# Gated tiles written in place, branch work dealt out anew, and the matrix state read ahead of the gating

## What is computed

```python
pool_y, pool_new = pool_mixer(cols(OFF_POOL, BRANCH_W), ...)      # branch 0
sb_y = stick_breaking(q_sb, k_all, v_all, pos0)                   # branch 1: 8 heads of 128
h_ml, c_new, n_new, m_new = mlstm_chunkwise(q_ml, k_ml, v_ml, ...)# branch 2: 4 heads of 256
for bi, yb in enumerate((pool_y, sb_y, ml_y)):
    gated = yb * silu(cols(OFF_Z + bi * BRANCH_W, BRANCH_W))
    term = sigmoid(cols(OFF_GATE + bi * D_MODEL, D_MODEL)) * (gated @ w_branch[bi])
    merged = term if merged is None else merged + term
y = merged @ w_out
x_out = x + rmsnorm(y, g_post)
```

## Time and profile before

| | |
|---|---|
| median of 3 runs | 2428.11 us (2427.13 to 2431.63) |
| the profiled execution's own time | 2423.55 us |
| its span | 2422.0 us |
| PE busy in the span | 2274.7 us, 94% |
| DVE, ACT, POOL busy | 61%, 38%, 10% |
| PE's share of the chain that ended last | 86% |

### The profile page before, as it was taken

One profiled execution on the slowest core, in us unless ns is written; L12 is line 12 of the kernel. 1 busy time (PEld: TensorE's weight loads), 2 busy tenths in 40 slices (PEclk: granted clock), 3 DMA queues, 4 the chain that ended last, 5 costly groups with the idle time before them and its releaser, 6 DMA issues.

```text
span 2422.0 us, 40440 instructions
## 1 busy us (share of the span) xinstructions
PE 2274.7 (94%) x16616; PEld 2233.8 (92%) x16616; DVE 1471.9 (61%) x1636; ACT 923.9 (38%) x1232; POOL 244.4 (10%) x301
## 2 busy tenths in 40 slices
PE   3799999999999999999999999999997898699996
PEld 3799999999999999999999999999886788699996
DVE  5867678667666666676666666655663666243333
ACT  4344334334433344444444444445541233122221
POOL 3100000000100001110000000003442111000000
PEclk7899999999999999999999999999997999899998
DMA  5244434444544444444444444466555553635322
GB/s 148 58 120 116 133 101 118 131 117 131 125 115 122 124 117 117 124 123 114 129 126 115 119 124 117 117 212 203 174 183 170 188 162 118 170 104 183 86 70 95
DMA packets 417613, 316.01 MB, mean 130 GB/s; under 512 B 11309, under 2 KB 376997, under 8 KB 415472
## 3 DMA queue, kind: packets, MB, share of 16 engines
q1 hardware_dynamic: 397456, 250.12, 37.4%
q0 software_dynamic: 20000, 63.61, 7.5%
HBM read 252.42 MB, written 61.26 MB: 130 GB/s over the span
## 4 chain that ended last, share of the span: by engine, by line
PE 86%; DVE 6%; DMA 4%; ACT 2%; issue 1%; POOL 1%; SPq 0%; DVEq 0%; ACTq 0%; POOLq 0%
PE pp L685 62%; PE pp L819 10%; PE pp L987 7%; DMA gt_lo<-gated_scratch 2%; PE M L693 2%; PE M L872 1%; PE M L902 1%; DMA raw_b<-in_w_out_dram 1%; PE M L919 1%; PE M L842 1%; PE M L785 1%; PE M L852 1%; DVE den L1867 1%; DVE xa L1427 1%; DVE XA L1750 0%
## 5 line engine op out<-in xcount | busy, mean ns | idle before, releaser
L685 PE MATMUL pp<-xa,wa_hi 128*128 128x288 f32 x7680 | 1543.6, 296 | 26.6 <-DVE wa_lo L1384 14.8
L685 PEld LDWEIGHTS pp<-xa,wa_hi 128*128 128x128 f32 x7680 | 1235.2, 188 | 29.0 <-DVE xa L1427 10.8
L685 PE MATMUL pp<-xa,wa_lo 128*128 128x288 f32 x3840 | 1131.6, 295 | 0.0
L685 PEld LDWEIGHTS pp<-xa,wa_lo 128*128 128x128 f32 x3840 | 725.9, 189 | 0.0
L1384 DVE TENSOR_TENSOR wa_lo<-raw_a,wa_hi 128x1024 fp32r<-128x1024 f32 x274 | 340.6, 1246 | 253.6 <-ACT wa_hi L1025 253.5
L1025 ACT ACTIVATE wa_hi<-raw_a 128x1024 fp32r<-128x1024 f32 x274 | 289.1, 1056 | 225.4 <-PE pp L685 218.6
L1384 DVE TENSOR_TENSOR wa_lo<-raw_r,wa_hi 128x1024 fp32r<-128x1024 f32 x136 | 173.2, 1273 | 141.6 <-ACT wa_hi L1025 141.6
L819 PE MATMUL pp<-gt_hi,wb_hi 128*128 128x288 f32 x768 | 171.9, 306 | 37.6 <-DMA gt_lo<-gated_scratch 37.6
L1025 ACT ACTIVATE wa_hi<-raw_r 128x1024 fp32r<-128x1024 f32 x136 | 143.5, 1055 | 133.5 <-PE pp L685 133.5
L819 PE MATMUL pp<-gt_hi,wb_lo 128*128 128x288 f32 x768 | 166.4, 299 | 0.0
L819 PE MATMUL pp<-gt_lo,wb_hi 128*128 128x288 f32 x768 | 166.4, 299 | 0.0
(11 more groups left out here) (278 smaller groups left out, 2137.3 us busy)
## 6 DMA issues: line engine op xcount, KB each, us to landing
raw_a<-in_w_in_dram SPq DMA_DIRECT2D x206, 512.0 KB, 5.0
raw_r<-in_w_in_dram SPq DMA_DIRECT2D x68, 512.0 KB, 4.9
z_scratch<-zs POOLq DMA_DIRECT2D x60, 576.0 KB, 3.3
raw_b<-in_w_branch_dram SPq DMA_DIRECT2D x48, 512.0 KB, 4.2
raw_b<-in_w_out_dram SPq DMA_DIRECT2D x32, 512.0 KB, 4.4
gz<-z_scratch SPq DMA_DIRECT2D x48, 288.0 KB, 4.0
gt_hi<-gated_scratch SPq DMA_DIRECT2D x6, 1152.0 KB, 10.3
gt_lo<-gated_scratch SPq DMA_DIRECT2D x6, 1152.0 KB, 13.1
```

The costliest lines, as they stand in the source:

```text
L685: i = nc.tensor.matmul(out, ws[:, slot, k, :], xa[:, o, part, k, :], start=opens and k == 0 and s == 0, stop=k == HK - 1 and s == 2, skip_ ...
```

## The change

- Tiles 6 and 7 of branch 1 and of branch 2 no longer go through DRAM. ACT and DVE write them into `gt_hi`, `gt_lo` (`gated_hi_direct`, `gated_lo_direct`), once the last segment of the branch before is done. `seg(16, 1)` and `seg(32, 1)` wait for them one by one; `gated(1, 1)` and `gated(2, 1)` load two tiles in place of four.
- A new semaphore `gt_free` counts the first halves: `seg(15, 0)` and `seg(31, 0)` raise it, and `gated(1, 0)`, `gated(2, 0)` wait for it and no longer for all segments of the branch. To make that early, the last two tiles of a branch run as (14, 0), (15, 0), (14, 1), (15, 1), and likewise 30 and 31.
- The segments are dealt out anew (`SB_SEGS`, `ML_SEGS`, `ML_SLOTS`): one stands ahead of head 0's transposes, head 1 comes after three in place of four, one segment each stands ahead of the last `weigh_values` and `sums_after` of head 6 and 7. The ML heads get 8, 8, 7, 7 segments, and head 3 has none behind its state products.
- `states` becomes a buffer of its own name at the place of `W_ml`. DVE copies the new state before the gating, `decay_rows(i)` moves to the start of head i and waits for the stores of the state, and the two splits of a head's gated tiles move into the next head. ACT's exponential of `W_ml` moves behind the copies to `mk_hi`.
- POOL masks `W_ml` first, then stores the last head's gated tiles, then multiplies `zml` and `oml`.
- In the last 16 tiles the splits of the first two tiles of the output projection move ahead of the last two merges.

```diff
+SB_SEGS = [(h, s) for h in range(H_POOL, H_SB - 2) for s in range(2)] + [(14, 0), (15, 0), (14, 1), (15, 1)]
+ML_SEGS = ([(16, 1), (17, 1)] + [(h, s) for h in range(H_SB + 2, H_ML - 2) for s in range(2)]
+           + [(30, 0), (31, 0), (30, 1), (31, 1)])
+ML_SLOTS = [[2, 1, 1, 2, 1, 1], [2, 1, 1, 2, 1, 1], [2, 1, 1, 1, 1, 1], [2, 1, 1, 2, 1, 0]]
...
+        states = sb("states", R + 82944, [P, 2 * MC * MDH])
-        states = num[:, :, :].rearrange("p c t -> p (c t)")
...
             def gated(b, s):
+                k0, k1 = 4 * s, KW - 2 if s and b else 4 * s + 4
...
-            sp.wait_ge(wb_used, H_SB)
+            sp.wait_ge(gt_free, 1)
             sp.wait_ge(g_stored, 32 * (PG + 4))
             gated(1, 0)
+            merge_gate(18)
+            weights(19)
+            head_past_v(SBH - 1)
+            sp.wait_ge(wb_used, H_SB)
+            sp.wait_ge(g_stored, 32 * (PG + SB_STORED))
+            gated(1, 1)
             merge_gate(19)
...
+            sp.wait_ge(gt_free, 2)
+            sp.wait_ge(g_stored, 32 * (PG + SB_STORED + 4))
+            gated(2, 0)
             sp.wait_ge(wb_used, H_ML)
-            sp.wait_ge(g_stored, 32 * (PG + SBH + 4))
-            gated(2, 0)
-            sp.wait_ge(g_stored, 32 * (PG + SBH + 2 * MLH))
+            sp.wait_ge(g_stored, 32 * (PG + SB_STORED + ML_STORED))
             gated(2, 1)
...
+                direct = {H_SB: PG + SBH, H_ML: PG + SBH + MC * MLH}
                 for k in range(4 * s, 4 * s + 4):
+                    if h in direct and k >= KW - 2:
+                        pe.wait_ge(glo_ready, direct[h] - (KW - 1 - k))
...
+            def gated_hi_direct(k, h, tile, src):
+                act.wait_ge(g_ready, k + 1)
+                act.wait_ge(wb_used, h)
+                nc.scalar.activation(gt_hi[:, tile, :], src, ACT.Copy).then_inc(ghi_ready, 1)
...
+                if i:
+                    k = MC * i - 1
+                    gated_hi(PG + SBH + k, PG + SB_STORED + k, zml[:, 1, :])
...
+            def gated_lo_direct(k, tile, src):
+                dve.wait_ge(ghi_ready, k + 1)
+                nc.vector.tensor_tensor(gt_lo[:, tile, :], src, gt_hi[:, tile, :].bitcast(F32), ALU.subtract
+                                        ).then_inc(glo_ready, 1)
...
             for t in range(KD):
-                h = H_ML + t + 2
-                if h < H_OUT:
-                    split_lo(At(h))
+                split_lo(At(H_ML + t + 2))
                 merge(H_ML + t)
                 if t >= 2:
                     merged_lo(t - 2)
-            split_lo(At(H_OUT))
-            split_lo(At(H_OUT + 1))
...
             def ml_head(i):
+                pool.wait_ge(W_ready, i + 1)
+                apply_mask(W_ml, ML_MASKED).then_inc(Wm_ready, 1)
+                if i:
+                    for c in range(MC):
+                        store_gated(PG + SBH + MC * (i - 1) + c, 2 * KW + MC * (i - 1) + c)
                 pool.wait_ge(mo_loaded, 16 * (i + 1))
                 pool.wait_ge(mg_loaded, 16 * (i + 1))
                 nc.gpsimd.tensor_tensor(zml[:, :, :], zml[:, :, :], oml[:, :, :], ALU.mult).then_inc(zg_ready, 1)
```

More of the change, by code:

```diff
@@ L139, in product_at, with ml_segs, ml_halves @@
     return p.times(7, 2 + j)
+def ml_segs(i, step):
+    at = sum(sum(x) for x in ML_SLOTS[:i]) + sum(ML_SLOTS[i][:step])
+    return ML_SEGS[at:at + ML_SLOTS[i][step]]
+def ml_halves(i, steps):
+    done = []
+    for step in steps:
+        done += [h for h, s in ml_segs(i, step) if s == 1]
+    return done
 def stored_before(p):
@@ L563, in _ @@
             ml_o(0)
-            for i in range(SBH):
+            head_past_k(1)
+            weights(4)
+            for i in range(1, SBH):
                 if i + 1 < SBH:
                     head_past_k(i + 1)
-                weights(2 * i + 4)
-                if 2 * i + 3 >= 4:
-                    merge_gate(2 * i + 3)
+                weights(2 * i + 3)
+                merge_gate(2 * i + 2)
+                if i == 1:
+                    head_qk(2)
                 if i + 2 < SBH:
@@ L624, in _ @@
             ml_c0(0)
+            ml_z(0)
             for i in range(MLH):
@@ L876, in sums_after, with next_seg @@
                               for j in range(NT)]).then_inc(after_done, 1)
-            for i in range(SBH):
+            segs = iter(SB_SEGS)
+            def next_seg():
+                seg(*next(segs))
+            next_seg()
+            keys_to_tokens(0)
+            next_seg()
+            scores(0)
+            next_seg()
+            keys_to_tokens(1)
+            next_seg()
+            scores(1)
+            next_seg()
+            sums_after(0)
+            next_seg()
+            for i in range(2, SBH):
                 keys_to_tokens(i)
-                seg(2 * i, 0)
+                next_seg()
                 scores(i)
[L882 to L888, removed]
+                next_seg()
+                weigh_values(i - 2)
+                next_seg()
+                sums_after(i - 1)
+                next_seg()
+            next_seg()
             weigh_values(SBH - 2)
+            next_seg()
+            sums_after(SBH - 1)
             seg(H_SB, 0)
-            sums_after(SBH - 1)
             seg(H_SB + 1, 0)
@@ L1808, in decay_rows, with merges @@
                 last.then_inc(D_ready, 1)
+            def merges(i, *after):
+                for h in ml_halves(i, after):
+                    merge(h)
+            KTR, SCORES, VTR, WEIGH, SSQ, STATE = range(6)
             def ml_head(i):
                 h = H_SB + 4 * i
-                steps.begin(0, 5)
+                steps.begin(0, 3 + MC)
+                decay_rows(i)
                 dve.wait_ge(mkhi_ready, i + 1)
@@ L1884, in ml_head @@
                                                ).then_inc(state_ready, 1)
+                dve.wait_ge(zg_ready, i + 1)
+                for c in range(MC):
+                    steps.link(nc.vector.tensor_tensor(num[:, c, :], num[:, c, :], den[:, :], ALU.mult))
+                    nc.vector.scalar_tensor_tensor(zml[:, c, :], num[:, c, :], hnorm[:, i * MC + c:i * MC + c + 1],
+                                                   zml[:, c, :], ALU.mult, ALU.mult).then_inc(g_ready, 1)
                 steps.end(1)
-                gated_lo(PG + SBH + MC * i + 1, zml[:, 1, :])
-                merge(h + 3)
-            decay_rows(0)
             for i in range(MLH):
                 ml_head(i)
+            for c in range(MC):
+                gated_lo_direct(PG + SBH + MC * (MLH - 1) + c, ML_STORED + c, zml[:, c, :])
+            merges(MLH - 1, STATE)
             def merged_lo(t):
```

198 lines of the change are left out of this document (99 added, 99 removed).

## The result

The changed kernel takes **2386.12 us** (median of 4 runs, 2384.08 to 2388.48), the kernel before, on the same chip, 2429.87 us (4 runs, 2427.13 to 2434.62): a ratio of 0.982, interval [0.981, 0.983], so 1.8% or 44 us faster. The forecast was 2381 us, in a range of 2369 to 2394. The profiled execution took 2387.73 us where the sum of the prediction had 2376.5: 11.2 us more, and nearly all of it sits in one term.

A forecast was written before the change was run, and what follows sets the result against it. PE was taken to bound the kernel, with gains only in its waits and slow clock: 3.7 - 19.5 - 4.0 - 6.6 - 4.2 - 13.0 - 3.5 = -47.1 us. From 2423.55 that gives 2376.5, plus 4.6 for the median: 2381, range 2369 to 2394.

The forecast's parts named there:

- opening of the SB heads: Start of SB heads: head 2 starts 2.8 us earlier, but two segments fewer (6.5 us) are done: +3.7 us.
- SB seam, waits: End of SB heads: extra segments shrink the `XD` waits, first and second reload waits go: -19.5 us.
- ML heads, waits: ML heads: state-copy waits (15.0 us) go, waits for the `W_ml` product and a weight tile come (8.4): -6.6 us.
- last reload: Load of branch 2's gated operand: asked for behind the merge of tile 31, wait falls from 24.5 to 11.5: -13.0 us.
- output projection: Start of the output projection: first two splits come ahead of the last merges, so its wait goes: -3.5 us.
- slow clock: PE's lowered clock behind long waits goes: -4.0 us at the SB end, -4.2 us at ML heads 1 and 3.
- forecast's own range of 2374 to 2389: Whole kernel: the likeliest case, centred on 2381 us, given chance 0.53.
- Landing takes 8.2 to 11.5: Branch 2's gated operand: us for its load to land, giving a PE wait of 10.3 to 13.6 us.
- a last load waited for over 18 us: Branch 2's gated operand: a PE wait this long was one of the stated signs that the forecast is wrong.
- rival of late weights: ML heads 1 and 2: weight tiles land 4 to 5 us later (+9), small stores slow last load (+4): 2394, chance 0.21.
- late weights of ML head 2: ML head 2, with one filler segment less: the weight tile comes behind DVE's need, costing some 2.4 us.
- A port shared by POOL and DVE: ML heads: POOL's product blocks DVE's `S_lo` on PE's path, 2.0 us in each of three heads: 2387, chance 0.11.

The follow-up runs named there:

- product-first kernels: Changed kernel with last load asked early (2363.45 us), second `gated_lo` and merges behind the `W_ml` product: 2366.79 us; head 0's merge kept ahead, `c0` loaded before `zml`: 2362.35 us.
- f_no_small: Changed kernel without the two 4 KB stores of `n_out` and the waits for them, output n left unwritten: 2379.72 us, ratio 0.979.
- u_state_behind: Changed kernel with the ML state read from PSUM behind the gating, still into its own buffer: 2390.89 us, ratio 0.984.
- a_small_late: Changed kernel with `n_out` in its own 64 bytes and its two 4 KB stores issued after the output projection's operand is built: 2387.28 us, ratio 0.9825.

## Why the prediction was right, and where it was not

The steps, each as PE's wait in us, expected and measured:

| step | expected | measured | from |
|---|---|---|---|
| opening of the SB heads | +3.7 | +3.6 | `qkv`, `issue`, `XA`, `XC_lo`: 8.0 before, 11.6 after |
| SB seam, waits | -19.5 | -19.4 | `XD` 8.4 to 2.1, reloads 13.1 to 0 |
| ML heads, waits | -6.6 | -7.5 | 15.0 to 6.6 + 0.6 + 0.3 |
| last reload | -13.0 | **-1.8** | 24.5 to 22.7 |
| output projection | -3.5 | -3.4 | 4.7 (the 3.5 and one of 1.2 further on) to 1.3 |
| slow clock | -8.2 | -6.4 | PE busy 2274.7 to 2268.3 |

One wait of the kernel before is in no row, 0.9 us ahead of the state products (for `den`); it is gone too. With it the measured column sums to -35.8, the distance between the two profiled executions, against -47.1 expected.

**What was right.** The seam's waits came out to the tenth of a us, and two parts of it were tried alone: without the early request it costs 7.6 us, without the direct tiles 16.4. In the ML heads the wait for the state copies is gone and the chain into the product of `W_ml` took its place with 1.92, 2.05 and 2.65 us where 2.0 a head was expected. The product-first kernels show that this is the round trip of the first gated tile, since those waits vanish when DVE no longer stands at the second one (and at the merge behind it, 1.5 us); ACT waits 5.5 to 6.1 us there for the store to land, against 5.19 in the earlier trace rows. The load of the last operand stood where the sum put it, behind the merge of tile 31, and once it is asked for early, 23 us go. The median of 2386.12 lies in the forecast's own range of 2374 to 2389, 5.1 us above the 2381. Some of that closeness is luck: the profiled execution before lay 4.6 us under its median and the one after 1.6 above its own, and those 6.2 us hide more than half of the 11.2 by which the sum was off.

**What was mis-sized.** The step that failed is "Landing takes 8.2 to 11.5" in the last reload: the mechanism and the place held, the landing took 20.4. The prediction saw the old load's 17.5 us and the stores' 12.8 beside it, and set them aside because the stores "now start about 2.5 us behind it". They start 3.5 us behind `gt_lo`'s issue, but that load needs 11.3 us even without them (f_no_small), so a lead of 3.5 is no protection; the data rate falls at 2035, and what is left then takes 10 us more. A lead of 6.5 us was enough in u_state_behind. By its own test (a last load waited for over 18 us) this step is wrong. It was priced in the rival of late weights, at +4 only; the stores are worth +9.2 at the wait, and the other 2.0 lie within the bounds given, 13.5 in 10.3 to 13.6.

Two smaller terms missed as well. The late weights of ML head 2 were put at 2.4 us and came to 0.6. And the sum took the slow clock's end at -8.2 but put nothing for the clock behind the waits that it expected itself: at 0.57 and 0.69 for 4 us each, ML heads 2 and 3 give back some 1.7 and 1.2 us (an estimate, 4 us times the share not granted). The opening stands at 0.83 over 20 us, where the kernel before has 0.91 over as many (1630:1650).

**What nearly happened.** Late weights: ACT's wait for `raw_b` is there, but in the changed kernel it costs PE 0.6 us; it costs 4.5 when the waits ahead of it are taken away. A port shared by POOL and DVE: POOL's product and DVE's split beside it,

```profile
1899.56 3.89 POOL L2243 TENSOR_TENSOR zml<-zml,oml 128x1152 f32<-128x1152 f32 x1 [3.18 <-DMA zml<-z_scratch]
...
1902.23 2.30 DVE L1768 TENSOR_TENSOR wb_lo<-raw_b,wb_hi 128x1024 fp32r<-128x1024 f32 x1
```

took 3.89 and 2.30 us against 2.62 and 1.22, but not on PE's path. `S_lo`, which is on it, did meet POOL's product in ML heads 1 to 3, as this rival has it; but it began 0.21, 0.11 and 0.17 us before the product and kept its 1.56 us, while the product took about 1.3 us more than before. That it came first by so little was luck; what it would have cost in the other order no run shows. The Trainium skill (SBUF — State Buffer, Who interferes with whom) has such a conflict, and these rows agree with it; its price for PE in this kernel was nothing.

**What stays open.** The last 1.2 us between the 9.2 of f_no_small's wait and the 8.0 between the profiled executions were not followed. Whether the stores' cost lies in their element size or in their queue wasn't tried; against the queue alone speaks that in a_small_late the two state stores of 256 KB ran on the same queue beside the same load, at 306 to 413 GB/s. That the waits of the opening and of head 2 are both bound by chains over several engines rests on one exchange each.

## What to carry to other kernels

A transfer's landing time belongs to what shares the DMA engines with it: take it from a row in the same place, with the same company, before one from elsewhere; two stores of 4 KB in elements of 4 bytes cost 9.2 us, in which the 326 GB/s of the window before move 3 MB, and moving them only helps if nobody waits for a transfer where they go. Read an experiment by its waits, not by its time alone: here a store moved late and a state read moved back gave times that spoke for the wrong theory. When a wait is gone and the time stays, ask what stood 2 us behind it; three of the edits tried here only handed the wait to the next engine.

## What the hardware showed that was not expected

Two stores of 4 KB each, in elements of 4 bytes, brought the data rate of all 16 DMA engines from 326 down to 26 GB/s for 3 us at a DMA share of 1.25 (56 GB/s at 0.83 in the next 3), and added 9.2 us to PE's wait for a load of 1152 KB that was already under way. The load was in SP's hardware queue and the stores in POOL's software queue, so separate queues gave no shelter. With 3.5 us of lead for the load they cost 9.2 us; with 6.5 the load landed in 11.8 us, against 11.3 without any such stores.
